# Half of every expert dot product from a DRAM table, for token blocks 2 and 3

## The reference

```python
q = (hb @ w_q).reshape(tb, PEER_HEADS, 2, PEER_HALF)
s = jnp.einsum('thcd,hcnd->thcn', q, keys)
...                                   # top-16 of s gives idx (token, head, 16) and gate
u = jnp.take(u_tab, idx, axis=0)
act = jax.nn.gelu(jnp.einsum('thkd,td->thk', u, hb).astype(jnp.float32), approximate=False)
w = (gate * act).astype(hb.dtype)
return jnp.einsum('thk,thkd->td', w, jnp.take(v_tab, idx, axis=0))
```

## Time and profile before

| | |
|---|---|
| median of 3 runs | 4306.65 us (4301.36 to 4309.41) |
| span of the profiled execution | 4304.1 us (the profile gives no time of its own for it beyond the span; the median is 2.6 us above) |
| TensorE, VectorE, ScalarE, GpSimd busy | 86%, 62%, 20%, 18% |
| DMA | 1530.03 MB, 355 GB/s over the span |
| mean granted TensorE clock | 0.965 |

### The profile page before, as it was taken

One profiled execution on the slowest core, in us unless ns is written; L12 is line 12 of the kernel. 1 busy time (PEld: TensorE's weight loads), 2 busy tenths in 40 slices (PEclk: granted clock), 3 DMA queues, 4 the chain that ended last, 5 costly groups with the idle time before them and its releaser, 6 DMA issues. The chain is left out here.

```text
span 4304.1 us, 39451 instructions
## 1 busy us (share of the span) xinstructions
PE 3720.8 (86%) x13650; PEld 2242.8 (52%) x13650; DVE 2660.6 (62%) x3879; ACT 881.0 (20%) x2023; POOL 780.9 (18%) x525
## 2 busy tenths in 40 slices
PE   9999999999999989766799697858888887777776
PEld 3444489446766677563687586334444443322222
DVE  3232368103999999974767877876666664444444
ACT  2233210101222121142111111122222222212112
POOL 0000000000233323332221311321211121212111
PEclk9999999999999999888899898879999999999999
DMA  3111258888999999999999999999999999999998
GB/s 134 59 59 59 72 184 302 301 314 308 379 412 400 390 404 421 404 382 392 421 413 427 418 417 426 426 419 424 419 428 428 429 418 428 418 426 429 428 428 373
DMA packets 136876, 1530.03 MB, mean 355 GB/s; under 512 B 15296, under 2 KB 15424, under 8 KB 15936
## 3 DMA queue, kind: packets, MB, share of 16 engines
q0 software_dynamic: 73728, 1073.77, 59.3%
q1 hardware_dynamic: 61488, 445.33, 27.0%
q10 hardware_dynamic: 1552, 9.57, 0.6%
HBM read 1524.42 MB, written 4.19 MB: 355 GB/s over the span
## 5 line engine op out<-in xcount | busy, mean ns | idle before, releaser
L1780 PE MATMUL bank<-arena_h,wring 128*128 128x128 f32 (+5 forms) x6656 | 1386.6, 372 | 113.4 <-DVE arena_h L1477 45.9
L1780 PEld LDWEIGHTS bank<-arena_h,wring 128*128 128x128 f32 x6656 | 1028.8, 196 | 469.0 <-issue 189.1
L636 POOL DMA_INDIRECT arena_c<-in_peer_uv,arena_c x256 | 513.8, 2007 | 2467.4 <-DVE arena_o L1409 1314.4
L1400 DVE SCALAR_TENSOR_TENSOR arena_c<-arena_c 128x2048 f32<-128x2048 f32 x256 | 587.1, 2293 | 173.4 <-DMA arena_c<-in_peer_uv,arena_c 173.2
L2172 PE MATMUL bank<-arena_c,arena_h 128*128 128x512 f32 x1020 | 481.1, 616 | 154.3 <-ACT arena_h L1006 154.3
L1409 DVE SCALAR_TENSOR_TENSOR arena_o<-arena_c,arena_o 128x2048 f32<-128x2048 f32 x234 | 551.0, 2355 | 46.0 <-ACT arena_c L806 40.6
L2139 PE MATMUL bank<-arena_c,cols 128*128 128x512 f32 x1024 | 471.5, 604 | 93.4 <-ACT cols L964 92.2
L1677 DVE SCALAR_TENSOR_TENSOR arena_c<-arena_c 128x2048 f32<-128x2048 f32 x128 | 293.4, 2292 | 335.0 <-DMA arena_c<-in_peer_uv,arena_c 334.9
L804 ACT ACTIVATE arena_c<-arena_c 128x1 f32<-128x1 f32 x384 | 78.0, 203 | 1915.9 <-DVE arena_c L1400 1427.5
L649 POOL DMA_INDIRECT arena_c<-in_peer_uv,arena_c x256 | 265.0, 1035 | 1030.7 <-PE bank L2139 520.8
L1621 DVE SCALAR_TENSOR_TENSOR arena_c<-arena_c 128x2048 f32<-128x2048 f32 x128 | 293.4, 2292 | 237.1 <-DMA arena_c<-in_peer_uv,arena_c 236.2
(11 more groups left out here) (237 smaller groups left out, 2622.4 us busy)
## 6 DMA issues: line engine op xcount, KB each, us to landing
wring<-in_w_in SPq DMA_DIRECT2D x176, 1024.0 KB
wring<-in_w_out SPq DMA_DIRECT2D x48, 1024.0 KB
wring<-in_peer_w_q SPq DMA_DIRECT2D x48, 1024.0 KB
wring<-in_gla_w_o SPq DMA_DIRECT2D x32, 1024.0 KB
wring<-in_conv_w_pw SPq DMA_DIRECT2D x32, 1024.0 KB
wring<-in_w_v SPq DMA_DIRECT2D x16, 1024.0 KB
wring<-in_w_ga SPq DMA_DIRECT2D x16, 1024.0 KB
wring<-in_w_o_quarters SPq DMA_DIRECT2D x16, 1024.0 KB
```

Source lines behind the costliest of these rows:

```text
L636: pool.indirect_dma_start(out=slot_of(n), out_offset=None, in_=uv_tab, in_offset=at)\
L1400: V.scalar_tensor_tensor(row, row, 1.0, block_of(h2, n // P), ALU.mult, ALU.mult, accum_out=act_u[:, n % TOP:n % TOP + 1]).then_inc(dotted, 1)
L1780: last = M(ps[bank][:, at:at + hi - lo], w_tile(slot)[:, k, :], act_in[:, k, lo:hi], start=k == 0, stop=k == KT - 1)
```

## The change

Three things change together.

1. **A table.** The host also lays out the first 1024 columns of U transposed (`peer_u_tiles`, 64 tiles of 1 MB) and the rest of U beside V (`peer_uv_rest`, 3072 float32 a row, 12 KB). While steps P+86 to P+140 (214 to 268) run, TensorE multiplies h2 of blocks 2 and 3 (256 tokens) with all 16384 half rows of U, in 32 groups of 512 experts; ScalarE copies each group's two banks to SBUF and writes them to an internal DRAM table `dots` (256 x 16384 float32).
2. **Half steps.** The first head of block 2 (steps 256 to 271) stays whole, with its V added by VectorE. From step 272 each step gathers, with two indirect DMAs, one number per token from `dots` and a 12 KB row; VectorE's dot product covers 1024 columns, and the number comes in as the bias of Gelu. V is split: TensorE adds columns 0 to 1023 (two matmuls), VectorE columns 1024 to 2047 (`add_row`, `add_half`), one step late, and a slot is free when both are done (`row_used` and `sum_used`).
3. **The mixer of blocks 2 and 3 earlier:** a pair each 3.5 steps rather than 5, the norm at P+73, the first query at P+82. Steps 234 to 271 have their V added by VectorE rather than TensorE. The loops of ScalarE and VectorE over block 2, and VectorE's over block 3, are written out.

```diff
-M2_AT, M2_EVERY = P + 4, 5
-X2_AT = P + 46
-RES2_AT = (P + 85, P + 89, P + 93, P + 97)
-NORM2_AT = P + 98
-QUERY2_AT = P + 109
-SUMS_FROM = P + 106
+M2_STEPS = tuple(P + 4 + 7 * n // 2 for n in range(16))
+X2_AT = P + 34
+RES2_AT = (P + 62, P + 65, P + 69, P + 72)
+NORM2_AT = P + 73
+QUERY2_AT = P + 82
+QUERY17_AT = P + 84
+DOTS_STEPS = tuple(P + 86 + 7 * g // 4 for g in range(GROUPS))
...
+            for n in range(2):
+                pool.wait_ge(u_out[n], 16 * GROUPS // 2)
+            def half_row(idx, idx_a, m, k, s):
+                pool.indirect_dma_start(out=act_a[:, k:k + 1], out_offset=None, in_=dots_flat,
+                                        in_offset=column(idx_a, m, k)).then_inc(uv_ready[s], 16)
+                pool.indirect_dma_start(out=uv_row[s][:, 0:ROW2], out_offset=None, in_=uv2_tab,
+                                        in_offset=column(idx, m, k)).then_inc(uv_ready[s], 16)
...
+                        hold(pool, row_used, i * 2 * TOP + (STEPS + n + 1), pool_passed)
+                        hold(pool, sum_used, i * 2 * TOP + (STEPS - WHOLE + n + 1), pool_passed)
+                        half_row(idx_cur2, idx_dot2, m, k, n % SLOTS)
...
+            def dots_out(g):
+                m = g % 2
+                act.wait_ge(u_mm, g + 1)
+                if g >= 2:
+                    act.wait_ge(u_out[m], 16 * (g // 2))
+                for b in range(NB2):
+                    A(dots_sb[:, m, b * 512:b * 512 + 512], ps[4 + 2 * m + b][:], ACT.Copy).then_inc(u_ev, 1)
+                act.wait_ge(u_ev, 2 * g + 6)
+                act.dma_start(dots_d[:, :, g * 512:g * 512 + 512],
+                              dots_sb[:, m, :].rearrange("p (b e) -> p b e", e=512)).then_inc(u_out[m], 16)
...
                     dot(s)
...
+                    if s > WHOLE:
+                        add_row(s - 1)
                     beside(s)
                     for part in topk:
                         part(k)
...
+            def dot_group(first, i, per, m, count):
+                pe.wait_ge(u_ev, count)
+                for t in range(2):
+                    tile_ready(first + t, i, per)
+                    for k in range(QUART):
+                        kk = t * QUART + k
+                        for b in range(NB2):
+                            last = M(ps[4 + 2 * m + b][:], h2T2[:, kk, b * P:b * P + P], w_quart(first + t)[:, k, :],
+                                     start=kk == 0, stop=kk == KT // 2 - 1)
```

More of the change, by code:

```diff
@@ L635, in _ @@
                         pool.wait_ge(s_ev, 2 * (BEHIND_HEAD[n] + 1))
[L636 to L650, removed]
@@ L1569, in _, with parts_at, after @@
             chain.step(V.memset(upad1[:, :, PAD + T1:], 0.0))
-            for U in range(2 * PH):
+            def parts_at(steps, find_softmax):
+                find, softmax = find_softmax
+                def after(k):
+                    if k in steps:
+                        find[steps.index(k)]()
+                    if k == GATE_OUT_AT:
+                        softmax()
+                return after
+            for U in range(SIDE):
                 topk = []
@@ L1590, in _ @@
                     if k == COPY_AT:
-                        indices(U + 1)
-                    if s < SUMS_FROM and not takes:
-                        add_row(s)
-            def add_sums(b, bank, free):
-                for q in range(4):
-                    dst = x2[:, 4 * q:4 * q + 4, b * P:b * P + P]
-                    ins = V.tensor_tensor(dst, by_tile(ps[bank + q][:]), dst, ALU.add)
-                ins.then_inc(free, 1)
-            def close_block1():
-                dve.wait_ge(uv_used, SLOTS)
-                add_sums(1, 4, mix1_free)
-                dve.wait_ge(mix1_free, 1)
+                        if U < SIDE - 1:
+                            indices(U + 1)
+                        else:
+                            indices2(0, SIDE)
@@ L1650, in hand_over @@
[L1650 to L1655 removed]
+                dve.wait_ge(mix1_free, 1)
             def final_means(blocks):
@@ new lines, in dot_groups @@
+            def dot_groups(first, done, count):
+                with pe.Fori(0, count // 2) as i:
+                    for m in range(2):
+                        dot_group(first + 2 * m, i, 4, m, i * 4 + (2 * done + 2 * m + 2))
+            whole_query(2 * PH, SB_WQ2)
+            head_scores(2 * PH, 0, NB2, qh2)
+            whole_query(2 * PH + 1, SB_WQ2 + 2)
+            for m in range(2):
+                dot_group(SB_U2 + 2 * m, None, 0, m, 2 + 2 * m)
+            head_scores(2 * PH + 1, 0, NB2, qh2)
@@ new lines, in _, with residual, sums @@
+            dot_groups(SB_U2 + 4, 2, EARLY_GROUPS - 2)
+            whole_query(2 * PH + 2, SB_WQ18)
+            dot_groups(SB_U2_REST, EARLY_GROUPS, GROUPS - EARLY_GROUPS)
+            head_scores(2 * PH + 2, 0, NB2, qh2)
+            def residual(b, bank):
+                for q in range(2):
+                    M(ps[bank + q][:], ident[:], x2[:, 4 * q:4 * q + 4, b * P:b * P + P], start=True, stop=False)
+            def sums(bank, weights, s, count, stop):
+                for q in range(count):
+                    last = M(ps[bank + q][:], weights, uv_row[s][:, HALF + q * 512:HALF + q * 512 + 512],
+                             start=False, stop=stop)
+                return last
@@ new lines, in _ @@
+            pe.wait_ge(u_ev, 4 + 2 * GROUPS)
+            pe.wait_ge(row_used, SLOTS + WHOLE)
+            residual(2, 4)
+            for s in range(WHOLE, STEPS):
+                U, k = s // TOP, s % TOP
+                pe.wait_ge(diag1_ready, s - WHOLE + 1)
+                sums(4, diag1[:, s % SLOTS, :], s % SLOTS, 2, s == STEPS - 1).then_inc(sum_used, 1)
+                if U >= SIDE - 2:
+                    continue
+                tile = SB_WQ19 + 2 * (U - WHOLE_UNITS)
+                first = (k - QUERY_FROM) * QUERY_STEP
```

338 lines of the change are left out of this document (169 added, 169 removed).

## The result

The changed kernel takes 4407.86 us (median of 4 runs, 4404.93 to 4409.72), the kernel before 4304.09 in the same session: ratio 1.0237, 95% interval 1.0222 to 1.0251. It is slower by 104 us; 23 were forecast. The direction and the first 3305 us came out as forecast, the half steps did not.

The account below looks back on a forecast made before the run. It took DMA bytes to bound the kernel: from 4304, -98 bytes, +36 numbers, +27 block 1, +15 block 2, +33 block 3's loop, +7 query tiles and rounding gave a 4324 us span, 4327 by the median; range 4235 to 4415.

Parts of the forecast that it names:

- Bytes, pairs, table, steps 132 to 271: Up to step 272's dot product: 83.9 MB more put it at 3283, handovers 16 us and steps 200 to 213 11: 3310.
- rival 3: Table stage: TensorE at clock 0.84 paces the table, 526 us against 472, +54, total 4381; chance 0.08.
- rival 4: Table's write: 2 KB rows to lines of 64 KB are slow, at half rate 39 us more, 4366; chance 0.05.
- The numbers in the queues: Half steps: each number's element packets and semaphore writes cost the DMA 0.15 us a step, 36 us over 240 steps.
- The cycle of a slot: Half steps: dot product n to n+4 takes one step (tau) + 11.0 in block 2, and must be within 4 tau.
- 6.0 to the dot product: Term of a slot's way in half steps: descriptors written to dot product, 7.2 less 1.2 us for fewer bytes.
- Descriptors: "2.2": Term of a slot's way in block 3: GpSimd's two descriptor writes of 0.94 us and 0.3 between.
- Block 2's slack: Block 2: 1.2 us slack at 4.06 a step; top-k 4 us late loses about 2.5 in six units, 15 us.
- Sums not late: Half steps: TensorE's sums (two matmuls, 1.7 us) end over 3 us before VectorE's release, not last even at half clock.
- Rival 2: GpSimd paces the half steps, two blocked writes and two register waits: 4.6 us in block 3, 4.35 in block 2, 4407; chance 0.17.
- Rival 1: Half steps: the DMA queue never runs dry, only bytes count: 4217 to 4253, say 4245; chance 0.30.
- the 1.15 of the upper bound: Block 3: descriptor writes starting inside VectorE operations wait, adding up to 1.15 us to a slot's cycle, 0.38 a step.

Follow-up runs that it names:

- five slots: Changed kernel with its four 16 KB slots divided into five of 12 KB for half steps, loops of blocks 2 and 3 written out: 4257.2 us, ratio 0.9893 to kernel before.
- add at once: Changed kernel with VectorE adding its half of V in the step's own turn, not a step late: 4386.13 us, ratio 1.0186 to the kernel before.
- constant waits: Changed kernel with GpSimd's loop over block 3 written out, so it waits on constants, not registers: 4381.22 us, ratio 1.0173 to the kernel before.
- two numbers: Changed kernel with each half step gathering its number twice, the second into columns nobody reads: 4564.45 us, ratio 1.0616 to the kernel before.
- numbers ahead: Changed kernel with each number's gather issued before GpSimd waits for the slot, with its own semaphores: 4322.70 us, ratio 1.0043 to the kernel before.
- ahead and at once: Changed kernel, four slots: number gathers before the slot wait, VectorE's add in the step's own turn, GpSimd waiting on constants: 4293.92 us, ratio 0.9982 to kernel before.
- five slots with numbers ahead: Changed kernel with five 12 KB slots and each number's gather issued ahead of the wait for its slot: 4256.37 us, ratio 0.9902 to the kernel before.

## Why the prediction was off, by its own steps

The forecast of the span, 4324, and the measured 4408 differ by 84 us: -5 to step 272, +41 in block 2 (511 for 470), +48 in block 3 (579 for 531), 0 at the end (12.7 for 13).

- **Bytes, pairs, table, steps 132 to 271: right in sum** (3304.9 for 3310), in its parts by luck. The bytes of these steps grew by 83.7 MB (83.9 forecast). The loss beyond them grew by 17 us where 27 were forecast, and step 132 itself came 6 us later. In steps 200 to 213 the losses were 2 us, not 11; but at the changeover GpSimd waited 20.5 us for the table's last write before it could gather the first half row: from step 268 to 272 33 us passed with bytes for 24, at a DMA share of 0.78, and no term had that. Share and clock were 1.00 while the table was made: rival 3 is out. Its write, 3476 packets of 2 KB in 2900 to 3100 us, took 84 ns each at 9% of the engines' time: rival 4 is out.
- **The numbers in the queues (0.15 us a step, 36 us): wrong**, they cost nothing that a run can tell. The nearest row was of another kind. A number's gather is 16 packets of 32 bytes at 13 ns, one an engine, 0.02 us a step with the semaphore writes. What a number costs is 1.28 us on GpSimd.
- **The cycle of a slot: the mechanism right, its size wrong; this is the step that failed.** The forecast had tau + 11.0 in block 2 and 11.8 to 12.4 in block 3; measured were tau + 13.7 in both. The mis-sized term is "6.0 to the dot product": it was 8.4 in block 2 (7.9 to landing, 0.5 to VectorE's turn) and 7.8 in block 3 (7.7 and 0.05). It came from one gather, taken as lonely; the dot product before it started at 3766.93, so even there the gather ahead had 1.9 us to run. The fastest rows of the change did land 5.7 us after their descriptors. But GpSimd's writes come unevenly, 3.5 to 6.5 us apart in block 3 (10th and 90th percentile of their ends), and at the end of a write the gather ahead has still 3.1 us to run on the mean. Rows whose predecessor had under 2.5 us left landed after 6.9 us, those with 3.5 to 5 left after 8.3. And some packets are slow: in 3900 to 4100 us a 12 KB packet takes 519 ns on the mean (median 460, 95th percentile 902), 473 with five slots.
- **Descriptors: "2.2" was 2.5**, as some writes are held up by VectorE; with the two register waits GpSimd started 0.98 us after its releaser, below the forecast's 1.2 to 1.8.
- **Block 2's slack.** The forecast took 1.2 us of slack at 4.06 us a step and charged 15 us for VectorE's late top-k. With 13.7 us for three periods there was no slack at all: in the first head of half steps they ran at 4.64 us already. The top-k's lateness is a part of the 13.7: 42 of block 2's 112 rows waited for VectorE, and the mean wait of 0.5 us, 0.05 in block 3, is worth some 15 us by a third a step (an estimate). In the last head of block 2, which has no top-k beside it, the steps took 4.31. By its own terms the forecast should have lost 4 less 1.2 = 2.8 us a head, not 2.5: 17 us, not 15.
- **"Sums not late"**: right for the change (six waits in block 3, 8.3 us). Once the add was no longer late, TensorE's sums and GpSimd's own writes came last, and the add at once could not bring what it seemed to.
- **Rival 2** gave 4407 and the time came to 4408, but not in its way. GpSimd is idle half of block 3, and five slots with the same two writes step at 3.87 us (block 3). Its second write counted as a part of the slot's way, a third of it a step. Rival 1 (4245) is what happens when that way has room: five slots gave 4257. Both lay in one condition, 3 tau against the way round, and the forecast had put that way 2.7 us too short in block 2 and 1.3 to 1.9 in block 3.

The Trainium skill (SBUF — State Buffer, the section on two separate sides), cited in the forecast, is seen again: at 4000.30 above the write takes 1.54 us where an undisturbed one takes 0.94, and ends 0.81 us after the dot product does at 4001.03. From 3000 us on in the change, 166 writes started inside one of VectorE's wide operations (dot products and adds above all), and 162 of them ended 0.81 to 0.87 us after it; 136 started before one and ran into it, and took their 0.95 us (median) as if alone. With 1210 ns a row's write in the change, that is 0.27 us of the way, not the 1.15 of the upper bound.

## What to carry to other kernels

When transfers get smaller, the buffers hide less: the latency and the engines' handshakes stay while the period shrinks. So write down the way of one buffer, from its landing to its next landing, and divide by the buffers; before an edit take each term from stretches in which the transfers are as crowded as they will be, not from a lonely one. And if a row shrinks, see whether the freed bytes make another buffer: here that, with constant waits, turned 2.4% slower into 1.1% faster. After such a change look for the limit that stands next: with one term of the way gone, the rows landed later and GpSimd's writes came last, so that 3.7 us less at one place were worth next to nothing.

## What the runs showed of the hardware that I had not expected

- An indirect gather of 4 bytes for each of 128 partitions is 16 packets of 32 bytes, 13 ns each, and is as dear on GpSimd as one of 12 KB rows: 0.94 us of descriptors, then 0.31 until the next can start. A third in the turn cost 2.6 us, not 1.25, since the gap before it was 1.09 and it then met the dot product.
- A descriptor write that starts inside a VectorE operation with two inputs in SBUF ends 0.81 to 0.87 us after it; one that starts before the operation is not held up.
- A wait on registers delayed GpSimd by 0.6 us more than one on a constant (0.98 in block 3 of the change, 0.40 in its block 2 and 0.36 in block 3 of the constant waits, from the add's end to the write). Two in a row cost little more than one: with one such wait, before, it was 1.0 us in the earlier trace rows and 0.81 on the median of block 3, counted from TensorE's end, which the profile models.
- 12 KB packets take 460 ns while the queue is full. In 3900 to 4100 us of the change 8% of them took over 700 ns, with five slots 0.4%; over block 3 of the change 28% of each gather's first 16 packets did, and 5% of the rest. Before, with a full queue, nine in ten of the 16 KB packets took 611 to 620. That an engine which had run out of work is the cause is read from their place, not tested apart.
- From the write of its descriptors to its landing a row took 6.9 to 9.5 us in block 3, by the kernel, though it was the same 1.5 MB each time: 6.89 with two numbers (period 5.11), 7.70 in the change (4.56), 8.11 with the numbers ahead (4.22), 9.47 with five slots (3.87). A ring gives back as waiting in the queue a part of what is saved elsewhere in it.
- TensorE's busy time hides how little it did. In 3830 to 4230 us it was busy 211 to 244 us in all changed kernels with half of V on it, but with 419 matmuls at a granted clock of 0.99 (five slots), 400 at 0.90 (ahead and at once), 355 at 0.80 (add at once) and 312 at 0.72 (two numbers): at the lower clock each takes longer. The count is not all of it, since the five slots with numbers ahead had 416 at 0.90; what decides is open. None of the times above hangs on it but the sums that came last in the add at once.
